# A triangular inverse that starts from eight-row blocks instead of two-row blocks, and a row statistic computed earlier

## The reference

```python
n = _rms_norm(h, attn_norm_w[l])
proj = jnp.einsum('bsd,dc->bsc', n, w_in[l])
...
m = jnp.where(strict, jnp.einsum('nbhik,nbhjk->nbhij', kb, kc) * decay, 0.0)
eye = jnp.eye(CHUNK, dtype=jnp.float32)
t_mat = lax.linalg.triangular_solve(eye + m, jnp.broadcast_to(eye, m.shape),
                                    left_side=True, lower=True, unit_diagonal=True)
u_base = jnp.einsum('nbhij,nbhjv->nbhiv', t_mat, vb)
w_mat = jnp.einsum('nbhij,nbhjk->nbhik', t_mat, kb * jnp.exp(gcum)[..., None])
qk = jnp.einsum('nbhik,nbhjk->nbhij', qc, kc) * decay
```

## Time and profile before

| | us |
|---|---|
| median of 3 runs | 1191.48 |
| lowest, highest | 1189.66, 1193.78 |
| the profiled execution, its whole time | 1187.83 |
| its span, first to last instruction | 1185.7 |
| TensorE busy (matmuls), share of the span | 1143.2, 96% |
| VectorE busy | 742.4, 63% |
| GpSimd busy | 518.8, 44% |
| ScalarE busy | 464.1, 39% |
| DMA over all queues | 97.26 MB, 82 GB/s |

### The profile page before, as it was taken

How to read it: one execution, slowest core, us unless ns; L and a number is a source line. 1 busy time by engine, 2 the same in 40 slices (tenths; PEclk the granted TensorE clock), 3 DMA queues, 4 the chain that set the end, 5 groups by cost and what they waited for, 6 DMA issues and landing times.

```text
span 1185.7 us, 15998 instructions
## 1 busy us (share of the span) xinstructions
PE 1143.2 (96%) x5834; PEld 910.6 (77%) x5834; DVE 742.4 (63%) x941; ACT 464.1 (39%) x812; POOL 518.8 (44%) x370
## 2 busy tenths in 40 slices
PE   6799999999999999999999999999999999999997
PEld 5576888978877777777778888876667768888775
DVE  5896854442485888888882112535764668886973
ACT  5335312124564223222323333434453543343653
POOL 4356412113164545554555445432237367532543
PEclk9899999999999999999999999999999999999999
DMA  8573331124132223232233223521123142122221
GB/s 229 73 111 58 54 54 37 36 87 92 36 98 81 88 90 106 71 106 86 91 106 98 97 98 98 152 72 36 36 72 105 38 124 72 37 72 72 71 72 71
DMA packets 101704, 97.26 MB, mean 82 GB/s; under 512 B 4880, under 2 KB 95760, under 8 KB 101264
## 3 DMA queue, kind: packets, MB, share of 16 engines
q1 hardware_dynamic: 101360, 95.97, 29.9%
q10 hardware_dynamic: 288, 0.52, 0.1%
HBM read 94.38 MB, written 2.10 MB: 81 GB/s over the span
## 4 chain that ended last, share of the span: by engine, by line
PE 62%; issue 16%; DVE 10%; POOL 8%; ACT 3%; DMA 1%; POOLq 0%; DVEq 0%; SPq 0%; ACTq 0%
PE ps L1799 16%; PE ps L1801 15%; PE ps L1800 15%; POOL w_lo L521 8%; PE ps L2312 4%; PE ps L2037 2%; PE ps L2030 2%; DVE kq L1225 1%; PE ps L2250 1%; PE ps L1991 1%; PE ps L2260 1%; DVE x_a L1178 1%; PE ps L2020 1%; DVE conv L1637 1%; PE ps L2144 1%
## 5 line engine op out<-in xcount | busy, mean ns | idle before, releaser
L521 POOL TENSOR_TENSOR w_lo<-raw,w_hi 128x512 fp32r<-128x512 f32 x332 | 472.9, 1437 | 645.9 <-ACT w_hi L634 631.8
L634 ACT ACTIVATE w_hi<-raw 128x512 fp32r<-128x512 f32 x332 | 197.5, 618 | 223.3 <-PE ps L1801 203.9
L1799 PE MATMUL ps<-x_a,w_hi 128*128 128x512 f32 x624 | 252.7, 405 | 19.9 <-POOL w_lo L521 17.2
L1800 PE MATMUL ps<-x_a,w_hi 128*128 128x512 f32 x624 | 244.4, 392 | 0.0
L1801 PE MATMUL ps<-x_a,w_lo 128*128 128x512 f32 x624 | 244.3, 392 | 0.0
L1799 PE MATMUL ps<-x_b,w_hi 128*128 128x512 f32 x416 | 165.3, 397 | 2.6 <-DVE y L1588 0.8
L1799 PEld LDWEIGHTS ps<-x_a,w_hi 128*128 128x128 f32 x624 | 118.0, 189 | 59.4 <-issue 33.1
L1801 PE MATMUL ps<-x_b,w_lo 128*128 128x512 f32 x416 | 162.3, 390 | 0.0
L1800 PE MATMUL ps<-x_b,w_hi 128*128 128x512 f32 x416 | 162.1, 390 | 0.0
L1800 PEld LDWEIGHTS ps<-x_a,w_hi 128*128 128x128 f32 x624 | 118.0, 189 | 25.0 <-issue 2.2
L1801 PEld LDWEIGHTS ps<-x_a,w_lo 128*128 128x128 f32 x624 | 117.8, 189 | 25.2
(11 more groups left out here) (341 smaller groups left out, 1625.2 us busy)
## 6 DMA issues: line engine op xcount, KB each, us to landing
raw<-in_w_up SPq DMA_DIRECT2D x44, 512.0 KB, 4.1
raw<-in_w_in SPq DMA_DIRECT2D x32, 512.0 KB, 8.1
raw<-in_c_w_in SPq DMA_DIRECT2D x24, 512.0 KB, 4.7
raw<-in_a_w_in SPq DMA_DIRECT2D x18, 512.0 KB, 4.8
raw<-in_w_down SPq DMA_DIRECT2D x16, 512.0 KB, 3.9
raw<-in_w_out SPq DMA_DIRECT2D x8, 512.0 KB, 4.0
raw<-in_c_w_out SPq DMA_DIRECT2D x8, 512.0 KB, 4.2
raw<-in_w_down SPq DMA_DIRECT2D x8, 384.0 KB, 3.6
```

What stands on the lines that cost most here:

```text
L521: nc.gpsimd.tensor_tensor(ring_half(WL, n), raw_half(n), f32(ring_half(WH, n)), SUB) \
L634: nc.scalar.activation(ring_half(WH, n), raw_half(n), ACT.Copy).then_inc(w_hi, 1)
L1799: mm(out, w_hi_, x_hi_, start=first, stop=False)
L1800: mm(out, w_hi_, x_lo_, start=False, stop=False)
```

## The change

The diff, cut to its core:

```diff
+BK = 8
+LEVEL_AT = {19: 2, 20: 3, 21: 4, 22: 5}
+FIRST_LEVEL = min(LEVEL_AT.values())
+T_AT = min(LEVEL_AT)
...
-        PAIRM = MASK[:, 2 * P:3 * P]
+        BLOCK = MASK[:, 2 * P:3 * P]
+        EYEB = MASK[:, 3 * P:3 * P + BK]
+        DQ = at("blocks_cut", [P, NB * H, 32], F32, AR + 73728)
+        DH = at("blocks_half", [P, NB * H, 16], F32, AR + 73728 + 2048)
+        DB = at("blocks", [P, NB * H, BK], F32, AR + 73728 + 3072)
+        XD = at("blocks_inv", [P, NB * H, BK], F32, AR + 73728 + 4096)
+        XS = at("row_spread", [P, NB * H, BK], F32, AR + 73728 + 5120)
+        XP = at("row_product", [P, NB * H, BK], F32, AR + 73728 + 6144)
...
-                if u == 18:
-                    gp.wait_ge(t2_ready, 1)
...
-                if u not in QUADS and u + 1 not in QUADS and u not in (U1 + 1, U2 + 1):
+                if u not in QUADS and u + 1 not in QUADS and u not in (U1 + 1, U1 + 2, U2 + 1):
...
             x_squares(6)
+            table(LN_EXP_SET)
+            split_hi(8)
+            rstd(0)
...
-                if u == 0:
-                    stat(0)
...
-                if u == 17:
+                if u in LEVEL_AT and u > T_AT:
+                    inverse_columns(LEVEL_AT[u])
+                if u in RET_GAP:
+                    ret_out(RET_GAP.index(u))
+                if u == T_AT - 1:
...
-                if 19 <= u <= 23:
-                    inverse_columns(u - 18)
...
+            def cut_blocks():
+
+                for r in range(0, P, 32):
+                    v.tensor_tensor(DQ[r:r + 32, :, :], M[r:r + 32, :, r:r + 32],
+                                    BLOCK[r:r + 32, r:r + 32].unsqueeze(1).broadcast_to([32, 16, 32]),
+                                    MUL).then_inc(blocks_cut, 1)
+                dve.wait_ge(blocks_cut, 4)
+                if BK == 8:
+                    step(v.tensor_tensor(DH[:, :, :], DQ[:, :, 0:16], DQ[:, :, 16:32], ADD))
+                    step(v.tensor_tensor(DB[:, :, :], DH[:, :, 0:8], DH[:, :, 8:16], ADD))
+                else:
+                    step(v.tensor_tensor(DB[:, :, :], DQ[:, :, 0:16], DQ[:, :, 16:32], ADD))
+                step(v.tensor_copy(XD[:, :, :], EYEB.unsqueeze(1).broadcast_to([P, 16, BK])))
+                step(v.tensor_tensor(XD[:, :, 0:1], XD[:, :, 0:1], DB[:, :, 0:1], SUB))
+
+            def eliminate(k):
+
+                w = k + 1
+                step(v.stream_shuffle(XS[:, :, :].rearrange("p a c -> p (a c)"),
+                                      XD[:, :, :].rearrange("p a c -> p (a c)"),
+                                      [i // BK * BK + k for i in range(32)]))
+                step(v.tensor_tensor(XP[:, :, 0:w], XS[:, :, 0:w],
+                                     DB[:, :, k:k + 1].broadcast_to([P, 16, w]), MUL))
+                step(v.tensor_tensor(XD[:, :, 0:w], XD[:, :, 0:w], XP[:, :, 0:w], SUB))
...
-                if u == 7:
+                if u == 8:
...
                 if u == 16:
                     dve.wait_ge(m_ready, 1)
-                    v.tensor_tensor(TT[:, :, :], M[:, :, :], PAIRM.unsqueeze(1).broadcast_to([P, 16, P]), MUL) \
-                        .then_inc(pair_ready, 1)
+                    cut_blocks()
+                    for k in range(1, BK - 1):
+                        eliminate(k)
+                        if BK == 16 and k in (4, 10):
+                            tile_done(16 + k // 10)
+                            rotate_tile(16 + k // 10)
                     v.tensor_tensor(T[:, :, :], T[:, :, :], UPPER.unsqueeze(1).broadcast_to([P, 16, P]), MUL) \
                         .then_inc(dt_ready, 1)
                     dve.wait_ge(dt_ready, 1)
...
                     dve.wait_ge(qk_filled, 1)
                     v.tensor_tensor(QKT[:, :, :], MX16, T[:, :, :], MUL).then_inc(qkt_ready, 1)
                     dve.wait_ge(qkt_ready, 1)
-                    dve.wait_ge(pair_ready, 1)
-                    v.scalar_tensor_tensor(out=T[:, :, :], in0=TT[:, :, :], scalar=-1.0,
-                                           in1=IDENT[:, :].unsqueeze(1).broadcast_to([P, 16, P]),
-                                           op0=MUL, op1=ADD).then_inc(t2_ready, 1)
-                if 18 <= u <= 23:
-                    level(u - 18)
+                    v.tensor_tensor(T[:, :, :].rearrange("p a (b c) -> p a b c", c=BK),
+                                    XD[:, :, :].unsqueeze(2).broadcast_to([P, 16, P // BK, BK]),
+                                    by_block(BLOCK), MUL).then_inc(t2_ready, 1)
+                if u in LEVEL_AT:
+                    level(LEVEL_AT[u])
...
-                    if k == 2 and midway is not None:
+                    if k == 0 and midway is not None:
                         stat(midway)
...
+            for _ in range(20):
+                mm(PS[:, 7, 0:P], ONES[:, :], ONES[:, :], start=True, stop=True)
...
-                elif u == 18 or u == 31:
+                elif u == T_AT or u == 31:
                     pe.wait_ge(bank_free, u - 3)
                     half_unit(2 * u, PS[:, u % 4, :], XA, 0, 4, True, False)
-                    if u == 18:
+                    if u == T_AT:
                         t_transposes()
...
-                if u == 6:
+                if u == 7:
...
-                if 18 <= u <= 23:
+                if u in LEVEL_AT:
                     heads = sum(g < u for g in RET_GAP)
                     if heads:
                         pe.wait_ge(ro_ready, heads)
                         pe.wait_ge(rs_ready, 4 * heads)
-                    level(u - 18)
+                    level(LEVEL_AT[u])
                 if u in RET_GAP:
-                    pe.wait_ge(upd_done, 4 * min(u - 17, 6))
+                    pe.wait_ge(qkt_ready, 1)
+                    if u >= T_AT:
+                        pe.wait_ge(upd_done, 4 * sum(g <= u for g in LEVEL_AT))
                     ret_head(RET_GAP.index(u))
```

More of the change, by code:

```diff
@@ L291, in build @@
         qkt_ready, t2_ready = sem("qkt_ready"), sem("t2_ready")
-        pair_ready = sem("pair_blocks_ready")
+        blocks_cut = sem("blocks_cut")
         tt_filled, tt_ready = sem("tt_filled"), sem("tt_ready")
@@ L731, in inverse_columns @@
                 for c in range(NB):
-                    act.wait_ge(t_filled, 4 * (l - 1) + c + 1)
+                    act.wait_ge(t_filled, 4 * (l - FIRST_LEVEL - 1) + c + 1)
                     t_, ps = (x.rearrange("p h (b two s) -> p h b two s", two=2, s=s)[:, :, :, 0, :]
@@ L1245, in level @@
                 s = 2 << l
+                n = 4 * (l - FIRST_LEVEL)
                 def half(ap, two):
@@ L1252, in level, with by_block @@
                 for c in range(NB):
-                    dve.wait_ge(xp_filled, 4 * l + c + 1)
+                    dve.wait_ge(xp_filled, n + c + 1)
                     v.tensor_tensor(half(XZ[:, c, :, :], 1), part(4 + c, 0), mask, MUL).then_inc(xs_ready, 1)
                 for c in range(NB):
-                    dve.wait_ge(txp_filled, 4 * l + c + 1)
+                    dve.wait_ge(txp_filled, n + c + 1)
                     u_ = half(TT[:, 4 * c:4 * c + 4, :], 1)
                     v.tensor_tensor(u_, u_, part(4 + c, 256), SUB).then_inc(upd_done, 1)
+            def by_block(ap):
+                return ap.rearrange("p (b c) -> p b c", c=BK).unsqueeze(1).broadcast_to([P, 16, P // BK, BK])
+            def cut_blocks():
[19 more added lines that the diff above has]
+                step(v.tensor_tensor(XD[:, :, 0:w], XD[:, :, 0:w], XP[:, :, 0:w], SUB))
             def ret_scores(h):
@@ L1380, in _ @@
                 elif u < 24:
-                    rotate_tile(u)
+                    if BK == 8 or u > 17:
+                        rotate_tile(u)
                 else:
@@ L2005, in t_transposes @@
                 pe.wait_ge(t2_ready, 1)
+                if T_AT > RET_GAP[0]:
+                    heads = sum(g < T_AT for g in RET_GAP)
+                    pe.wait_ge(ro_ready, heads)
+                    pe.wait_ge(rs_ready, 4 * heads)
                 for a_ in range(16):
@@ L2013, in level @@
                 s = 2 << l
+                n = 4 * (l - FIRST_LEVEL)
                 def half(ap, two):
                     return ap.rearrange("p (b two s) -> p b two s", two=2, s=s)[:, :, two, :]
-                if l > 0:
+                if n > 0:
                     for c in range(NB):
-                        pe.wait_ge(upd_done, 4 * (l - 1) + c + 1)
+                        pe.wait_ge(upd_done, n - 4 + c + 1)
                         for h in range(H):
@@ L2022, in level @@
                 for c in range(NB):
-                    if l == 0 and c == 0:
+                    if n == 0 and c == 0:
                         pe.wait_ge(t2_ready, 1)
                         pe.wait_ge(tt_ready, 1)
-                    if l > 0:
-                        pe.wait_ge(t_taken, 4 * (l - 1) + c + 1)
+                    if n > 0:
+                        pe.wait_ge(t_taken, n - 4 + c + 1)
                     for h in range(H):
@@ L2033, in level @@
```

(7 more changed lines are left out.)

2 lines of the change are left out of this document (removed).

## The result

| | before | after |
|---|---|---|
| median, range (4 runs each) | 1191.31 (1189.66 to 1193.78) | 1175.68 (1173.4 to 1177.84) |
| ratio to before, 95% interval | | 0.987 (0.9851 to 0.9889) |
| profiled execution, whole time | 1187.83 | 1173.4 |

A forecast was written before the change was run, and what follows sets the result against it. TensorE was taken to bound the opening and mixer, working back to back except for 19 us of waits. 3.3 + 18.1 - 6.4 = 15.0 us, taken off the median of 1191.48, gave 1176.5; range 1169 to 1185.

The forecast's parts named there:

- Opening, 3.3 us predicted: Opening: unit 5 ends 2.0 us earlier, the columns' wait of 1.3 us ends; 3.3 us gained in sum.
- Leaving TensorE, 18.1 us predicted: Doublings: two fewer with transposes save 17.6 us, one wait behind a doubling 0.5; all on the path, 18.1 us.
- VectorE's chain: VectorE after M: starting block ready 16.2 us later if undisturbed; with GpSimd's meetings the first doubling reached 32 us after M.
- Seven meetings: VectorE operations lengthened by about 1.0 us beside GpSimd's nine cuts, 34 to 42: seven taken, 6.9 us; bounds 3.4 and 10.9.
- The cost on TensorE, 6.4 us predicted: First doubling: VectorE's meetings make it end at 170.1 instead of 163.7, 6.4 us later.
- a fall of the clock at the first is hidden: TensorE idling before the transposes may lower its clock, at no cost, as VectorE is last at the second product.
- the second predicted wait: First doubling: TensorE waits for VectorE again, 1 to 3 us between the two products.
- (a): Rival: every GpSimd cut blocks VectorE in full; cost 10.9 us, gain 10.5, time 1181; chance 0.17.
- (b): Rival: few meetings, GpSimd cutting quickly between short operations; cost 3.4 or less, gain 18.0, time 1173.5; chance 0.20.
- (c): Rival: the clock falls at TensorE's idle places and returns late; 1.8 us each time, twice 3.7; 1180; chance 0.08.
- (d): Rival: opening gains nothing as the statistic waits behind half 8, possibly landing late; gain 13.0, time 1178.5; chance 0.05.
- (e): Rival: slower, all 26 new VectorE operations pay 1.0 us each; cost 27.5 against 21.4 gain, 1197.6; chance 0.03.

The follow-up runs named there:

- e1: Kernel before with only the opening's edits, the inverse left as it was: 1186.90 us, ratio 0.9978.
- e7: Kernel after, but ScalarE splits half 9 right after 1/rms and halves 10 to 14 earlier: 1171.97 us, ratio 0.9856.
- e11: e10 together with the earlier weight splits of e7: 1167.41 us, ratio 0.9822.
- e2: Kernel before with only the inverse's edits, the opening left as it was: 1179.23 us, ratio 0.9911.
- e3: Kernel after without the twenty products of ones ahead of the first weights: 1173.49 us, ratio 0.9868.
- e4: Kernel after, but GpSimd writes zeros instead of cutting the low parts of halves 34 to 42: 1165.90 us, ratio 0.9803.
- e9: Kernel before, unchanged, run again for a second trace: 1190.48 us.
- e5: Kernel after with nine products of ones on TensorE during the wait for the starting block, to keep the clock up: 1173.07 us, ratio 0.9863.
- e12: Kernel after, unchanged, run again for a second trace: 1173.64 us, ratio 0.9866.
- e6: Kernel after with transposes inside unit 20, doublings and heads 0 and 1 one unit later, tile 19's rotation behind the first doubling: 1175.46 us, ratio 0.9879.
- e10: Kernel after with e6's edits, but the transposes ahead of unit 20 instead of inside it: 1173.56 us, ratio 0.9861.
- e13: The kernel of e10 run once more: 1172.57 us, ratio 0.9855.

## Why the prediction was right, point by point

**Opening, 3.3 us predicted.** The traces have M 3.4 us earlier (134.3 to 130.8), e1's median 2.85. The stall moved into unit 4 as said (3.2 us; 4.4 predicted), 1/rms begins at 29.98 (30.0), unit 5 ends at 51.23 (51.2); the stall is shorter because TensorE came to it later, and half 9 was ready at 41.4 (41.2). Two pieces were off. The statistic's product came at 28.92, not 27.8: in after the granted clock is 0.92, 0.50, 0.50, 0.50 and 0.87 in the five windows of 1 us from 11, where in the trace of before the matmuls had their short pitch from 12.7 on; half 8's landing hid that. And the wait for the columns was priced at its own 1.3 us, while in two traces of three it also cost a fall of the clock of about 1.6. The first trace of before was a fortunate one: the three traces with the old opening have M at 134.3, 137.3 and 137.3, the nine with the new one (e7 and e11 apart) at 130.1 to 133.1. That makes the opening's part larger than 3.4 in most executions, as the 5.7 between e2 and e3 have it too. e1's median (1.4 to 3.8) doesn't show it: its trace completes M at 130.1 and loses 1.6 us at the scores, where the clock fell. Whether that happened in most of its runs isn't known. That 3.3 met the 3.4 of the first pair of traces was partly luck.

**Leaving TensorE, 18.1 us predicted.** e4, where VectorE doesn't hold TensorE up, has 1032.2 from M to end against 1051.4 and 1051.1: 19.0. The term was 0.9 too small. About 0.3 to 0.4 of it was a short wait in the middle of unit 17, the fourth of the four in the earlier trace rows, which the prediction doesn't mention:

```profile
141.16 0.47 PE L1799 MATMUL ps<-x_a,w_hi 128*128 128x512 f32 x1 [0.15 <-POOL w_lo L521]
```

The matmul ahead of it starts at 140.62, 0.54 us earlier instead of 0.227; e9 and e1 have the same gap, after and e4 don't. GpSimd's three cuts there take 7.93 us. The rest I can't place.

**VectorE's chain.** Undisturbed, the block was to be ready 16.2 us after M and the first doubling reached after 24.9; e4 shows 16.4 and 24.9. With the meetings, 32 was predicted and 32.3 measured. Seven meetings for 6.9 us were booked; of the nine cuts eight were met, for 7.4. The rule of the Trainium skill (SBUF — State Buffer, "SBUF: two separate sides"), a lock for the whole instruction, would have made it up to nine times 1.27. The rows agree with the lock itself: the copy and the product of 48 elements start 0.03 and 0.05 us after a cut and end 0.09 and 0.07 after that cut has ended, and GpSimd's cuts grow in their turn. The surcharge comes out below 1.29 because part of the operation's own time falls into the wait: 1.12 us for the copy at 138.41 against e4, 1.10 for the product at 141.15.

**The cost on TensorE, 6.4 us predicted.** It was 7.6: the second set of products begins 15.6 us after TensorE stood ready for the transposes (148.46 to 164.04) where e4 needs 8.0. This is the term that was mis-sized: 0.7 because VectorE was later by half a meeting and the slack was smaller than 0.5, and 0.5 because of the step "a fall of the clock at the first is hidden, since VectorE is last at the second". The fall cost TensorE 2.5 us, and it became the later of the two by 0.5. For the same reason the second predicted wait, 1 to 3 us between the two sets, isn't there: TensorE spent it at the lower clock level. e2 and e5 show VectorE last there, by 0.2.

**Sum.** Predicted 3.3 + 18.1 - 6.4 = 15.0; by these readings 3.4 + 19.0 - 7.6 = 14.8, where the two profiled executions differ by 14.4. The 15.6 between the medians come from the first chip alone; on e12's chip it is 14.6. From M to end the gain is 10.8, with 11.7 predicted. Two errors of about 1 us, in opposite directions, cancelled. The rivals: (a), every cut at full length, and (b), few meetings, fall by the count of eight and the 7.4 us (11.4 at full length, 3.9 for four meetings); (c) happened as a mechanism, with a fall at the first wait, at a quarter of its price of 1.8 since most of it was covered; (d) falls by e1, though e12, whose half 8 landed 1.2 us later than in after, shows that its mechanism is there; (e) fails since no cut meets two operations.

## What to carry to other kernels

A chain of small operations on VectorE is cheap until GpSimd works beside it on SBUF: count GpSimd's instructions in the stretch, not VectorE's, and price each at nearly its own length (here 1.0 to 1.1 us for one of 1.27 to 1.29), but for those beside operations that read PSUM. A wait of TensorE for a chain on another engine is a distance from the event that starts the chain; before more work is moved in front of it, look whether that work needs anything that stands behind the chain in the same queue (e6 against e10). And where an operation only removes a stall, ask what is bound next: 6.7 us at unit 5 were 2.5 at M.

## What the runs showed of the hardware

- **Whether the clock falls at a short wait varies from run to run.** A pause of 2.44 us ahead of the transposes left it up (e11), pauses of 2.54 and 2.55 didn't (e13, e10). At the scores, with the same waits of 1.6 and 1.1 us, it fell in 6 of 14 traces; from the last product with the probabilities to the pooling these have 8.9 to 10.3 us, the others 7.4. At the columns it fell in two of three. These falls, 1.5 to 2.9 us each, are as large as the differences between executions of one kernel.
- **A warm start is kept or not by small differences.** The 40 passes of ones end at 7.3 to 8.8 us, and the first weights come 0.9 to 2.5 us later. In the six traces where that pause is listed as 0.94, 1.13, 1.13, 1.19, 1.49 and 1.77 us (e1, e6, e7, e13, e11, e10) the clock is at 1.00 from 11 to 16 us; in the four with 2.06, 2.13, 2.15 and 2.52 (e5, e4, after, e12) it falls at 10.9 to 12.1, with TensorE at work again, and is back at 14.3 to 15.6. In these four the passes also took least time (6.1 to 6.7 us, against 6.9 to 7.7), so the pause alone isn't shown to decide it.
- **A meeting is paid once for each cut.** The surcharge is 0.95 to 1.12 us on an operation of 16 elements and on one of 512 alike, with one exception of 0.36 (at 160.49), and no operation behind it pays again. The product that reads PSUM kept its 2.28 us beside the cut at 148.78, and so did the shuffle of 0.74 that reads PSUM beside the one at 159.71; the short shuffles of SBUF data lay beside no cut, so nothing is shown of them.
